# An RWKV scan in chunks of 64 tokens: both directions in one batch, every product 64x64 in two diagonal tiles of the matrix engine

## The chip, the cores and the metric

One core of a Trainium2 chip runs the whole program in one launch. The metric is the device time of that launch in microseconds, the median of three runs.

## The reference

Two transformer-like blocks, one behind the other, over 512 tokens of width 1024, all in float32. The first has an RWKV-7 mixer and a gated linear attention, then a mixture of 32 experts; the second has a gated recurrence, a Hyena convolution, a conformer part and two mixtures of 16 experts. The change touches the RWKV mixer alone:

```python
def rwkv7_bidir_scan(r, w, k, v, kk, b):    # 8 heads of 64; k, w, b per direction
    ...
    def step(s, inp):
        r_t, w_t, k_t, v_t, kk_t, b_t = inp
        sa = jnp.einsum('dbhvk,dbhk->dbhv', s, -kk_t)
        s = s * w_t[..., None, :] + sa[..., None] * b_t[..., None, :] + v_t[..., None] * k_t[..., None, :]
        return s, jnp.einsum('dbhvk,dbhk->dbhv', s, r_t)
    _, ys = lax.scan(step, s0, xs)
    return ys[0] + jnp.flip(ys[1], axis=1)
```

Here w is `exp(-exp(-0.5) * sigmoid(...))`, k_dir is `k * (1 + (a - 1) * k_a)`, b is `kk * a`; the result is normalised per head, gets a bonus from `r * (k_dir[0] + k_dir[1]) * r_k`, and is gated.

## The kernel before, in words

Features lie on the partitions, tokens on the free axis: a tile [128, 4, 512] holds four pairs of heads (partitions 0 to 63 the one head, 64 to 127 the other, called `par` 0 and 1). The stages run one behind the other in blocks, each with a barrier at its end; the order within a block is that of each engine's own instructions, and semaphores join them.

`rwkv_keys` makes kk; `to_tokens` transposes v. Then, for each direction:

- `rwkv_direction` (L636): eight matmuls (L656) with 64 rows make the logits of decay and rate, ACT takes their sigmoid (L663), DVE scales them (L681), sums the decay over each chunk of 128 tokens by sixteen scans (L685), centres the sums on half a chunk (L691), and ACT takes three exponentials (L665 to L676). DVE forms kd and a·kk (L696 to L699) and the products q, b, k (L703 to L706); GpSimd keeps kd_sum (L712, L714) and makes r (L717).
- `to_tokens` transposes b and k (L736, evacuated by L744 and L751).
- `rwkv_scan` (L753) goes over four chunks of 128 tokens. In a chunk the inverse of a triangular 128x128 matrix per head is built up in seven levels of doubling. Jobs, each one PSUM bank, are put into one list. A, N, RB, BT and RK (L835) are products of two of q, r, k, b over 64 rows, four heads each, masked by DVE. At each level l: U = N·X (L839), then X (L843) and Z (L847), which add to one half of X and Z in place. rhs (L854, L855), sa (L861), y (L867 to L869) and S (L875, L876) carry the state; those of the chunk before are put between the levels of the next. PE waits until the job eight places before has left its bank and until the inputs' jobs are evacuated. DVE does all evacuations in list order and waits for its own last one each time (L893 to L925).

`rwkv_output` (L927) then normalises y; DVE multiplies kd_sum by r and r_k there (L978), while GpSimd splits the next projection's weights (L273). ACT takes a square root (L967), DVE the reciprocal (L980).

Float32 products appear in the trace as two MATMUL records each, every one with its own LDWEIGHTS record.

## Time and profile before

| | us |
|---|---|
| median of 3 runs | 3662.59 |
| lowest, highest | 3660.34, 3702.36 |
| profiled execution, its own time | 3687.77 |
| its span, first to last instruction | 3686.0 |
| PE busy (14568 matmul records) | 2898.9 |
| DVE busy | 1643.6 |
| ACT busy | 541.7 |
| GpSimd busy | 369.0 |
| mean granted clock of PE | 0.851 |

Times inside the program are read from the profiled execution, in us from its first instruction. Busy shares are means over very different stages, so a stage is read by its own window. PE is the matmul queue, PEld its weight loads; the clock 1.00 is 2.4 GHz and 0.50 is 1.2 GHz.

### The profile page before, as it was taken

To read this page: it belongs to the slowest core of one execution; us is meant where nothing else is said; L and a number is where in the kernel's file an instruction comes from. 1 tells how busy PE (TensorE), PEld (TensorE's weight loads), DVE (VectorE), ACT (ScalarE), POOL (GpSimd) and SP (SyncE) were. 2 spreads that over 40 slices of the span, in tenths; PEclk is the share of its full clock that TensorE was granted. 3 is DMA by queue.
4 is the path that set the end of the run, shared out by engine and by line. 5 is a ranking of instruction groups with operands and counts; after the bars stand their busy time and mean duration, and the time that the engine had idled before them with its cause. 6 is when DMAs were issued, how large, how long until landed. Compare 5 with 4: busy or idle time off the path is not lost. (4 is left out here: it accounts for less than half of the span.)

```text
span 3686.0 us, 35596 instructions
## 1 busy us (share of the span) xinstructions
PE 2898.9 (79%) x14568; PEld 1854.9 (50%) x14568; DVE 1643.6 (45%) x2393; ACT 541.7 (15%) x742; POOL 369.0 (10%) x143
## 2 busy tenths in 40 slices
PE   5873679969967899996378365689898676798997
PEld 4663378859846545453266134534343454443343
DVE  6967465465553323234577555422121584312123
ACT  2121100010011111111422201200000213100001
POOL 3312010010010000000322223000000230000000
PEclk8986579868977899998689577789999887799998
DMA  5650000000012699993164101279999310699995
GB/s 169 215 181 0 9 1 1 1 1 1 1 46 117 288 411 415 415 410 155 46 217 149 41 0 46 120 316 427 428 428 427 104 54 23 263 427 428 428 427 238
DMA packets 136674, 725.36 MB, mean 197 GB/s; under 512 B 11878, under 2 KB 67174, under 8 KB 99367
## 3 DMA queue, kind: packets, MB, share of 16 engines
q1 hardware_dynamic: 112632, 700.98, 47.0%
q10 hardware_dynamic: 23920, 22.68, 1.9%
q8 instruction: 85, 1.39, 0.2%
q14 instruction: 37, 0.30, 0.0%
HBM read 721.53 MB, written 2.10 MB: 196 GB/s over the span
## 5 line engine op out<-in xcount | busy, mean ns | idle before, releaser
L1631 PE MATMUL ps<-s_c_ring,s_c_XG 128*64 128x512 f32 x2048 | 475.0, 620 | 80.2 <-DMA s_c_ring<-in_exp_w 62.6
L289 PE MATMUL ps<-s_h_part,s_w_hi 128*128 128x512 f32 x944 | 310.5, 412 | 63.9 <-PEq L413 63.0
L1631 PEld LDWEIGHTS ps<-s_c_ring,s_c_XG 128*64 128x64 f32 x2048 | 164.5, 142 | 384.8 <-issue 383.7
L273 POOL TENSOR_TENSOR s_w_lo<-s_w_raw,s_w_hi 128x2048 fp32r<-128x2048 f32 (+1 forms) x46 | 213.1, 4638 | 1279.6 <-ACT s_w_hi L266 1250.3
L1744 DVE TENSOR_TENSOR s_c_hid<-ps,s_c_sil 128x512 f32<-128x512 f32 x32 | 34.3, 1072 | 515.7 <-PE ps L1631 515.7
L289 PEld LDWEIGHTS ps<-s_h_part,s_w_hi 128*128 128x128 f32 x944 | 186.7, 200 | 105.8 <-issue 65.6
L1672 PE MATMUL ps<-s_c_ring,s_c_hidT 128*64 128x512 f32 x1024 | 223.3, 594 | 0.0
L1631 PE MATMUL ps<-s_m_ring,s_m_XG 128*64 128x512 f32 x1024 | 222.9, 593 | 0.0
L345 DVE SCALAR_TENSOR_TENSOR s_mod_acc<-s_mod_w,s_mod_silu,s_mod_acc 128x512 f32<-128x512 f32 x196 | 189.2, 965 | 47.4 <-DMA s_mod_w<-in_w_mod 38.5
L289 PE MATMUL ps<-s_h_part,s_w_lo 128*128 128x512 f32 x472 | 191.8, 406 | 0.0
L289 PE MATMUL ps<-s_src_part,s_w_hi 128*128 128x512 f32 x384 | 123.0, 402 | 42.7 <-DVE s_src_part L1262 29.2
L1631 PEld LDWEIGHTS ps<-s_m_ring,s_m_XG 128*64 128x64 f32 x1024 | 72.9, 137 | 142.7 <-issue 141.6
L266 ACT ACTIVATE s_w_hi<-s_w_raw 128x2048 fp32r<-128x2048 f32 (+1 forms) x46 | 87.1, 1893 | 386.4 <-DMA s_w_raw<-in_w_out 270.3
L1672 PEld LDWEIGHTS ps<-s_c_ring,s_c_hidT 128*64 128x64 f32 x1024 | 72.1, 137 | 137.3 <-issue 136.0
L1756 DVE SCALAR_TENSOR_TENSOR s_c_Y_lo<-ps,s_c_w_slot,s_c_Y_hi 128x512 fp32r<-128x512 f32 x32 | 22.5, 746 | 211.6 <-ACT s_c_Y_hi L1713 211.6
L1672 PE MATMUL ps<-s_m_ring,s_m_hidT 128*64 128x512 f32 x512 | 113.4, 595 | 0.0
L839 PE MATMUL ps<-s_rw_X,s_rw_N 128*128 128x128 f32 x768 | 107.2, 298 | 5.6 <-DVE s_rw_Z L899 5.6
L1744 DVE TENSOR_TENSOR s_m_hid<-ps,s_m_sil 128x512 f32<-128x512 f32 x16 | 17.4, 1088 | 199.2 <-PE ps L1631 199.2
L289 PEld LDWEIGHTS ps<-s_src_part,s_w_hi 128*128 128x128 f32 x384 | 74.6, 195 | 60.6 <-DVE s_src_part L1262 30.8
L839 PEld LDWEIGHTS ps<-s_rw_X,s_rw_N 128*128 128x128 f32 x768 | 101.1, 212 | 7.7 <-DVE s_rw_Z L899 6.3
L289 PEld LDWEIGHTS ps<-s_h_part,s_w_lo 128*128 128x128 f32 x472 | 94.0, 199 | 20.9
L1563 DVE SCALAR_TENSOR_TENSOR s_xT<-ps,s_mod_l,s_xT 128x512 f32<-128x512 f32 x144 | 96.3, 740 | 2.0 <-PE ps L1555 1.8
(584 smaller groups left out, 4716.6 us busy)
## 6 DMA issues: line engine op xcount, KB each, us to landing
s_c_ring<-in_exp_w SPq DMA_DIRECT2D x192, 2048.0 KB, 17.3
s_m_ring<-in_moe_w_gate SPq DMA_DIRECT2D x32, 2048.0 KB, 12.0
s_m_ring<-in_moe_w_up SPq DMA_DIRECT2D x32, 2048.0 KB, 15.3
s_m_ring<-in_moe_w_down SPq DMA_DIRECT2D x32, 2048.0 KB, 12.4
s_mod_w<-in_w_mod SPq DMA_DIRECT2D x112, 512.0 KB, 5.0
s_w_raw<-in_w_in ACTq DMA_DIRECT2D x21, 1024.0 KB, 9.2
s_w_raw<-in_w_out SPq DMA_DIRECT2D x8, 1024.0 KB, 5.5
s_w_raw<-in_cf_w SPq DMA_DIRECT2D x16, 512.0 KB, 5.5
```

The lines of the kernel that those rows point to most:

```text
L266: nc.scalar.activation(self.hi[:, i % 2, :, at], self.raw[:, i % 2, :, at], ACT.Copy).then_inc(hi_done.sem, 1)
L273: nc.gpsimd.tensor_tensor(self.lo[:, i % 2, :, at], self.raw[:, i % 2, :, at], self.hi[:, i % 2, :, at].bitcast(F32), ALU.subtract).then_i ...
L289: last = nc.tensor.matmul(bank, w[a][:, i % 2, k, c0:c0 + P], x[b][:, k, at], start=start, stop=stop)
L345: ins = nc.vector.scalar_tensor_tensor(acc, w, c, acc, ALU.mult, ALU.add)
L839: last = mm(bank[:, h * P:(h + 1) * P], N[:, par, h, :], X[:, par, h, :], start=True, stop=True)
L1563: ins = nc.vector.scalar_tensor_tensor(xT[:, d, :], ps[:, bank, :], out_gate(d), xT[:, d, :], ALU.mult, ALU.add)
L1631: last = nc.tensor.matmul(ps[x * SLOTS:(x + 1) * SLOTS, bank + fh, :], XG[:, k, c0:c0 + SLOTS], w[x][:, at:at + 512], start=(k == 0), stop ...
L1672: last = nc.tensor.matmul(ps[rows, DOWN + half, :], hidT[:, f, rows], w[x][:, at:at + 512], start=(f == 0), stop=(f == nj - 1))
L1744: nc.vector.tensor_tensor(hid_out[:, fh * per:(fh + 1) * per, :], ps[:, UP + fh, :].rearrange("s (p j) -> s p j", j=nj), sil[:, fh * 512:( ...
L1756: nc.vector.scalar_tensor_tensor(Y_lo[:, at], ps[:, DOWN + half, :], w_slot[:], Y_hi[:, at].bitcast(F32), ALU.mult, ALU.subtract).then_inc ...
```

## The change

A chunk has 64 tokens and there are eight steps; the inverse has six levels, the first of them from masks. The backward direction is stored reversed, so both directions are the same program, and a job's eight blocks of 64 columns are (direction, pair of heads). Each block has two products, head 0 from partitions 0 to 63 into PSUM partitions 0 to 63, head 1 from 64 to 127 into 64 to 127. U, X and Z only compute the half that is used, 32 columns, one job per direction. b and k come to token order by products with a diagonal that holds the chunk's total decay; v by products with the identity. ACT evacuates b_tok, k_tok, v_tok, rhs, sa and y of the first four steps; DVE the rest, without waiting for itself; GpSimd makes the diagonals and the decayed state. A semaphore per engine takes the place of the shared ones. `rwkv_prepare` takes the place of both `rwkv_direction`s, `to_tokens` of v, b and k are gone from this part (the function stays for other stages), the multiplication of kd_sum by r and r_k goes from `rwkv_output` to the preparation's end, and X, Z, N, RB, RK and v_tok lie where r, k and kk were.

`rwkv_prepare`, ACT and DVE, for each direction d:

```diff
+                for j in range(2 * CT):
+                    c, name, dst = j % CT, (w0, ka0)[j // CT], (sg, a_)[j // CT]
+                    act.wait_ge(mm_done.sem, m0 + d * 2 * CT + j + 1)
+                    nc.scalar.activation(dst[:, c, :], ps[:, j, :], ACT.Sigmoid, bias=vcol(name, c)).then_inc(*act_out.up())
+                act.wait_ge(act_out.sem, a0 + d * PER_ACT + 2 * CT)
+                act.wait_ge(dve_out.sem, v0 + d * PER_DVE + 1)
+                for c in range(CT):
+                    ins = nc.scalar.activation(kd[:, c, :], a_[:, c, :], ACT.Identity, bias=keep[:, c:c + 1], scale=vcol("rw_k_a", c))
+                ins.then_inc(*act_out.up())
+                act.wait_ge(dve_out.sem, v0 + d * PER_DVE + 2)
+                nc.scalar.activation(flat(ex), flat(cc), ACT.Exp, scale=decay).then_inc(*act_out.up())
+                act.wait_ge(dve_out.sem, v0 + d * PER_DVE + 3)
+                nc.scalar.activation(flat(sg), flat(sg), ACT.Exp, scale=-decay).then_inc(*act_out.up())
+                act.wait_ge(act_out.sem, act_out.n)
+                nc.scalar.activation(flat(cc), flat(cc), ACT.Exp, scale=-decay).then_inc(*act_out.up())
+                act.wait_ge(act_out.sem, act_out.n)
+                ends = cc[:, :, 0:T:RW_CHUNK] if d else cc[:, :, RW_CHUNK - 1:T:RW_CHUNK]
+                to = tot[:, :, d * CT:(d + 1) * CT].rearrange("p n c -> p c n")
+                nc.scalar.activation(to[:, :, ::-1] if d else to, ends, ACT.Copy).then_inc(*act_out.up())
+                if d == 0:
+                    nc.scalar.activation(v_back[:, :, ::-1], v_[:, :, :], ACT.Copy).then_inc(*act_out.up())
...
+                for c in range(CT):
+                    dve.wait_ge(act_out.sem, ad + c + 1)
+                    x, s = (cc[:, c, ::-1], sg[:, c, ::-1]) if d else (cc[:, c, :], sg[:, c, :])
+                    ins = V.tensor_tensor_scan(x, reset, s, 0.0, ALU.mult, ALU.add)
+                ins.then_inc(*dve_out.up())
+                dve.wait_ge(dve_out.sem, vd + 2)
+                V.tensor_tensor(flat(sg), flat(cc), flat(sg), ALU.subtract).then_inc(*dve_out.up())
+                dve.wait_ge(act_out.sem, ad + 2 * CT + 1)
+                vlink(V.tensor_tensor(flat(kd), flat(kd), flat(k_), ALU.mult))
+                V.tensor_tensor(flat(a_), flat(a_), flat(kk), ALU.mult)
+                dve.wait_ge(act_out.sem, ad + 2 * CT + 2)
+                vlink(V.tensor_tensor(k, kd[:, :, :], ex[:, :, :], ALU.mult))
+                V.scalar_tensor_tensor(b, a_[:, :, :], -1.0, ex[:, :, :], ALU.mult, ALU.mult)
+                dve.wait_ge(act_out.sem, ad + 2 * CT + 3)
+                V.tensor_tensor(q, kk[:, :, :], sg[:, :, :], ALU.mult)
+                dve.wait_ge(act_out.sem, ad + 2 * CT + 4)
+                ins = V.tensor_tensor(r, r_[:, :, :], cc[:, :, :], ALU.mult)
+                if d == 1:
+                    vlink(ins)
+                    ins = V.tensor_tensor(flat(kd_sum), flat(kd_sum), flat(kd2), ALU.add)
+                ins.then_inc(*dve_out.up())
+            dve.wait_ge(dve_out.sem, v0 + 2 * PER_DVE)
+            for c in range(CT):
+                V.scalar_tensor_tensor(kd_sum[:, c, :], r_[:, c, :], vcol("rw_r_k", c), kd_sum[:, c, :], ALU.mult, ALU.mult)
```

`rwkv_scan`, the order of the jobs, and the matmuls of the wide and the small ones:

```diff
+jobs = [("A", 0, 0, 0), ("N", 0, 0, 0)]
+for j in range(N_STEP):
+    last = j > 0
+    for l in range(1, TOP + 1):
+        one, two = [], []
+        if l == 1:
+            one, two = [("rhs", j - 1, 0, 0)] if last else [], [("RB", j, 0, 0)]
+        elif l == 2:
+            one, two = [("sa", j - 1, 0, 0)] if last else [], [("BT", j, 0, 0)]
+        elif l == 3:
+            one, two = [("S", j - 1, 0, 0)] if last else [], [("b_tok", j, 0, 0)]
+        elif l == 4:
+            one, two = [("RK", j, 0, 0)], [("A", j + 1, 0, 0), ("N", j + 1, 0, 0)] if j + 1 < N_STEP else []
+        else:
+            one, two = [("k_tok", j, 0, 0), ("v_tok", j, 0, 0)], [("y", j - 1, 0, 0)] if last else []
+        jobs += [("U", j, 0, l), ("U", j, 1, l)] + one
+        for d in range(2):
+            jobs += [("X", j, d, l)] if l < TOP else []
+            jobs += [("Z", j, d, l)]
+        jobs += two
+jobs += [(name, N_STEP - 1, 0, 0) for name in ("rhs", "sa", "y")]
...
+def by_act(job):
+    return job[0] in ("b_tok", "k_tok", "v_tok", "rhs", "sa") or job[0] == "y" and job[1] < N_STEP // 2
...
+                if name in ("A", "N", "RB", "BT", "RK"):
+                    lhs, rhs_ = {"A": (qt, bt), "N": (bt, qt), "RB": (bt, rt), "BT": (kt, qt), "RK": (kt, rt)}[name]
+                    for h, (w, c) in enumerate(blocks):
+                        for r in rows:
+                            last = mm(bank[r, h * C:(h + 1) * C], lhs[r, w, c, at], rhs_[r, w, c, at], start=True, stop=True)
+                elif name in ("b_tok", "k_tok"):
+                    pe.wait_ge(pool_did.sem, 2 + 2 * j + 1)
+                    src = bt if name == "b_tok" else kt
+                    for h, (w, c) in enumerate(blocks):
+                        for r in rows:
+                            last = mm(bank[r, h * C:(h + 1) * C], src[r, w, c, at], diag2[j % 2][r, h, :], start=True, stop=True)
...
+                elif name == "U":
+                    after(*(("N", j, 0, 0) if l == 1 else ("X", j, d, l - 1)))
+                    for c in range(CT):
+                        h = d * CT + c
+                        for r in rows:
+                            last = mm(bank[r, c * (C // 2):(c + 1) * (C // 2)], N[r, h, :], part(X[r, h:h + 1, :], l, 0)[:, 0], start=True, stop=True)
+                elif name == "X":
+                    after("U", j, d, l)
+                    for c in range(CT):
+                        h = d * CT + c
+                        for r in rows:
+                            last = mm(bank[r, c * (C // 2):(c + 1) * (C // 2)], Z[r, h, :], part(U[l][r, h:h + 1, :], l, 0)[:, 0], start=True, stop=True)
+                elif name == "Z":
+                    after("U", j, d, l)
+                    for c in range(CT):
+                        h = d * CT + c
+                        for r in rows:
+                            last = mm(bank[r, c * (C // 2):(c + 1) * (C // 2)], U[l][r, h, :], part(Z[r, h:h + 1, :], l, 1)[:, 0], start=True, stop=True)
...
+                elif name == "y":
+                    after("RB", j, 0, 0)
+                    after("RK", j, 0, 0)
+                    after("sa", j, 0, 0)
+                    for h, (w, c) in enumerate(blocks):
+                        for r in rows:
+                            o = bank[r, h * C:(h + 1) * C]
+                            mm(o, S[r, h, :], rt[r, w, c, at], start=True, stop=False)
+                            mm(o, vt[r, h, :], RK[r, h, :], start=False, stop=False)
+                            last = mm(o, sa[r, h, :], RB[r, h, :], start=False, stop=True)
+                else:
+                    after("b_tok", j, 0, 0)
+                    after("k_tok", j, 0, 0)
+                    after("sa", j, 0, 0)
+                    for h in range(BLK):
+                        for r in rows:
+                            o = bank[r, h * C:(h + 1) * C]
+                            mm(o, k_tok[r, h, :], vt[r, h, :], start=True, stop=False)
+                            last = mm(o, b_tok[r, h, :], sa[r, h, :], start=False, stop=True)
+                last.then_inc(pe_did.sem, 1)
```

GpSimd's and DVE's part of it:

```diff
+        @block.gpsimd
+        def _(pool):
+            for l in range(1, TOP + 1):
+                ins = nc.gpsimd.memset(U[l][:], 0.0)
+            ins.then_inc(pool_did.sem, 1)
+            nc.gpsimd.memset(S2[0][:], 0.0).then_inc(pool_did.sem, 1)
+            pool.wait_ge(pool_did.sem, 2)
+            for j in range(N_STEP):
+                if j >= 2:
+                    pool.wait_ge(pe_did.sem, pe_at[("k_tok", j - 2, 0, 0)])
+                t = tot[:, j, :].unsqueeze(2).to_broadcast([P, BLK, C])
+                nc.gpsimd.tensor_tensor(diag2[j % 2][:], bcast(same, BLK), t, ALU.mult).then_inc(pool_did.sem, 1)
+                if j + 1 < N_STEP:
+                    if j > 0:
+                        pool.wait_ge(dve_did.sem, done_at[("S", j - 1, 0, 0)][1])
+                        pool.wait_ge(pe_did.sem, pe_at[("y", j - 1, 0, 0)])
+                    nc.gpsimd.tensor_tensor(S2[(j + 1) % 2][:], S2[j % 2][:], t, ALU.mult).then_inc(pool_did.sem, 1)
...
+                if name == "A":
+                    vlink(tt(X[:], banked(i), bcast(first, BLK), ALU.mult))
+                    ins = tt(X[:], X[:], bcast(same, BLK), ALU.add)
+                elif name == "N":
+                    tt(N[:], banked(i), bcast(strict, BLK), ALU.mult)
+                    vlink(tt(Z[:], banked(i), bcast(first_t, BLK), ALU.mult))
+                    ins = tt(Z[:], Z[:], bcast(same, BLK), ALU.add)
+                elif name in ("RB", "RK", "BT"):
+                    to, mask = {"RB": (RB, incl), "RK": (RK, incl), "BT": (BT, strict)}[name]
+                    ins = tt(to[:], banked(i), bcast(mask, BLK), ALU.mult)
+                elif name == "U":
+                    mask = level(l).rearrange("p (m b) -> p m b", b=2 ** l).unsqueeze(1).to_broadcast([P, CT, C // 2 ** (l + 1), 2 ** l])
+                    ins = tt(part(U[l][:, mine, :], l, 0), halves(i, l), mask, ALU.mult)
+                elif name in ("X", "Z"):
+                    M = part(X[:, mine, :], l, 0) if name == "X" else part(Z[:, mine, :], l, 1)
+                    ins = tt(M, M, halves(i, l), ALU.add)
+                elif name == "y":
+                    dve.wait_ge(act_did.sem, done_at[("y", N_STEP // 2 - 1, 0, 0)][1])
+                    for w in range(2):
+                        o = y_at(j, w)
+                        ins = tt(o, banked(i)[:, w * CT:(w + 1) * CT, :], o, ALU.add)
...
+                    dve.wait_ge(pool_did.sem, 2 + 2 * (j + 1))
+                    S = S2[(j + 1) % 2]
+                    ins = tt(S[:], banked(i), S[:], ALU.add)
+                ins.then_inc(dve_did.sem, 1)
```

`rwkv_output` loses its four passes:

```diff
-            for c in range(CT):
-                nc.vector.scalar_tensor_tensor(kd_sum[:, c, :], r_[:, c, :], vcol("rw_r_k", c), kd_sum[:, c, :], ALU.mult, ALU.mult).then_inc(*dve_out.up())
```

## Rows read from the trace of the kernel before

**Rows 1.** Windows by stage: us, busy (x records) by engine, PEclk, DMA share.

```profile
436.98:1053.46 616.48, 551.53 (x3952) 483.75 (x3952) 328.45 (x530) 32.49 (x37) 23.36 (x4) 0.83 0.00 1
441.90:477.65 35.75, 11.54 (x16) 4.19 (x16) 29.78 (x29) 12.62 (x13) 10.38 (x2) 0.54 0.00 0
484.36:746.21 261.85, 256.47 (x1920) 230.52 (x1921) 129.70 (x231) 0.01 (x1) 0.00 (x0) 0.88 0.00 1
...
791.68:1053.46 261.78, 256.41 (x1920) 230.41 (x1920) 129.67 (x231) 0.00 (x0) 0.00 (x0) 0.88 0.00 1
```

**Rows 2.** Timeline of the forward scan: start, us, engine, line, [idle <-releaser].

```profile
584.79 1.95 PE L839 MATMUL ps<-s_rw_X,s_rw_N 128*128 128x128 f32 x16
585.06 0.42 DVE L906 TENSOR_TENSOR s_rw_ex<-s_rw_ex,ps 128x256 f32<-128x256 f32 x1 [0.47 <-PE ps L847]
585.96 0.69 DVE L903 TENSOR_TENSOR s_rw_U<-ps,s_masks 128x512 f32<-128x512 f32 x1 [0.47 <-PE ps L839]
...
586.70 0.38 PE L843 MATMUL ps<-s_rw_U,s_rw_ex 128*128 128x128 f32 x1
```

**Rows 3.** PE's timeline, an S job (L875, L876) at full clock.

```profile
572.54 0.34 PE L875 MATMUL ps<-s_rw_sa,s_rw_lw 128*64 128x64 f32 x4
...
573.01 0.33 PE L875 MATMUL ps<-s_rw_sa,s_rw_lw 128*64 128x64 f32 x4
```

**Rows 4.** PE's timeline, an S job at half clock.

```profile
1050.78 0.48 PE L875 MATMUL ps<-s_rw_sa,s_rw_lw 128*64 128x64 f32 x4
...
1051.63 0.48 PE L875 MATMUL ps<-s_rw_sa,s_rw_lw 128*64 128x64 f32 x4
```

**Rows 5.** PE's timeline where A's and N's jobs meet.

```profile
486.02 0.27 PE L835 MATMUL ps<-s_rw_a,s_rw_q 64*128 64x128 f32 x1
486.02 0.27 PE L835 MATMUL ps<-s_rw_q,s_rw_a 64*128 64x128 f32 x1
```

**Rows 6.** PE's timeline, products with 32 moving columns at half clock.

```profile
1195.29 4.48 PE L1362 MATMUL ps<-s_Mboth,s_base 128*128 128x32 f32 x20 [5.99 <-DVE s_Mboth L1403]
```

**Rows 7.** Timeline of the first rwkv_direction.

```profile
441.93 4.71 PE L656 MATMUL ps<-s_proj,s_w2s 64*128 64x512 f32 x8 [1.28 <-PEq L725]
...
448.66 5.16 DVE L685 TENSOR_TENSOR_SCAN s_rw_cc<-s_base,s_rw_lw 128x128 f32<-128x128 f32 x16
...
453.50 0.69 ACT L663 ACTIVATE s_rw_a<-ps,s_vec 128x512 f32<-128x512 f32 x1 [1.02 <-PE ps L656]
...
454.21 1.28 ACT L665 ACT_TABLE_LOAD   x1
...
462.50 2.28 DVE L699 TENSOR_TENSOR s_rw_a<-s_rw_a,s_rw_kk 128x2048 f32<-128x2048 f32 x1
...
468.60 6.58 DVE L704 TENSOR_TENSOR s_rw_a<-s_rw_a,s_rw_ex 128x2048 f32<-128x2048 f32 x1
```

**Rows 8.** Timeline of rwkv_output.

```profile
1060.90 9.41 POOL L273 TENSOR_TENSOR s_w_lo<-s_w_raw,s_w_hi 128x2048 fp32r<-128x2048 f32 x2 [280.42 <-ACT s_w_hi L266]
1061.69 0.69 DVE L976 TENSOR_SCALAR s_gn_sq<-ps 128x512 f32<-128x512 f32 x1 [1.67 <-PE ps L952]
...
1062.30 9.88 DVE L978 SCALAR_TENSOR_TENSOR s_rw_kd_sum<-s_proj,s_vec,s_rw_kd_sum 128x512 f32<-128x512 f32 x4
...
1065.09 0.63 ACT L967 ACTIVATE s_gn_sq<-s_gn_sq 128x512 f32<-128x512 f32 x1
```

**Rows 9.** Groups of GpSimd: busy us, mean ns of one.

```profile
L2253 POOL TENSOR_TENSOR s_hY<-s_hU,s_Ks 128x512 f32<-128x512 f32 x4 | 6.8, 1706 | 0.0
...
L1586 POOL MEMSET s_c_GT<- 128x512 f32 x2 | 1.1, 526 | 0.0
```

**Rows 10.** Windows of PE alone: us, busy (x records), PEclk.

```profile
441.00:444.40 3.40, 2.47 (x6) 1.00 0.01 2
444.40:454.60 10.20, 9.07 (x11) 0.50 0.00 0
...
540.00:550.20 10.20, 10.20 (x47) 0.50 0.00 0
```

More of the change, by code:

```diff
@@ L30 @@
 GLA_CLAMP = 80.0
-LEVELS = 7
+RW_CHUNK, RW_LEVELS = 64, 6
 N_GROUPS, PER_GROUP = 4, 8
@@ L122, in shape_constants @@
     cols.add("base_end", np.zeros((P, 1)))
-    cols.add("strict", np.concatenate([row < col, row > col], axis=1))
     cols.add("incl", np.concatenate([row <= col, row >= col], axis=1))
+    tok, to = row % RW_CHUNK, np.arange(RW_CHUNK)[None, :]
+    cols.add("same64", tok == to)
+    cols.add("strict64", tok < to)
+    cols.add("incl64", tok <= to)
+    cols.add("level0", (tok // 2 == to // 2) & (tok > to))
+    cols.add("level0_t", (tok // 2 == to // 2) & (tok < to))
     levels = []
-    for back in (False, True):
-        for s in (2 ** l for l in range(LEVELS)):
-            lower = (row // (2 * s) == col // (2 * s)) & (row // s > col // s)
-            levels.append(lower.T if back else lower)
+    for s in (2 ** l for l in range(1, RW_LEVELS)):
+        lower = (tok // (2 * s) == to // (2 * s)) & (tok // s > to // s)
+        levels.append(lower[:, (to[0] // s) % 2 == 0])
     cols.add("levels", np.concatenate(levels, axis=1))
+    cols.add("reset", np.tile(np.arange(T) % RW_CHUNK != 0, (P, 1)))
     return cols
@@ L976, in _ @@
                         nc.vector.tensor_scalar(sq[:, 0, :], ps[:, 0, :], 1.0 / RW_HD, RW_GN_EPS, ALU.mult, ALU.add).then_inc(*dve_out.up())
-                        for c in range(CT):
-                            nc.vector.scalar_tensor_tensor(kd_sum[:, c, :], r_[:, c, :], vcol("rw_r_k", c), kd_sum[:, c, :], ALU.mult, ALU.mult).then_inc(*dve_out.up())
                         dve.wait_ge(act_out.sem, a0 + 1)
@@ new lines, in build, with again @@
+                        bufs = {n: sbuf(scan, "rw_" + n, [P, 2, CT, T]) for n in ("q", "r", "k", "b")}
+                        bufs["v_back"] = sbuf(scan, "rw_v_back", [P, CT, T])
+                        bufs["tot"] = sbuf(scan, "rw_tot", [P, T // RW_CHUNK, 2 * CT])
+                        rwkv_prepare(proj, kk, w2, a2, kd_sum, bufs, masks["reset"])
+                        def again(t, n):
+                            return [t.rearrange("p c n -> p (c n)")[:, m * T:(m + 1) * T].rearrange("p (h i) -> p h i", i=RW_CHUNK) for m in range(n)]
@@ new lines, in build @@
+                        old = again(proj[:, 0:8, :], 8) + again(kk[:, :, :], 4)
+                        for n in ("X", "Z", "N", "RB", "RK", "v_tok"):
+                            bufs[n] = [old.pop(), old.pop()]
+                        for n in ("S", "diag"):
+                            bufs[n] = [sbuf(scan, "rw_" + n, [P, 2 * CT, RW_CHUNK]) for _ in range(2)]
+                        bufs["U"] = {l: sbuf(scan, "rw_U", [P, 2 * CT, RW_CHUNK]) for l in range(1, RW_LEVELS)}
+                        for n in ("BT", "rhs", "sa", "b_tok", "k_tok"):
+                            bufs[n] = sbuf(scan, "rw_" + n, [P, 2 * CT, RW_CHUNK])
```

396 lines of the change are left out of this document (141 added, 255 removed).

## The prediction

> **What bounds the kernel now.** I read the core's span first, then the windows by stage, then the timeline of one stretch of the scan, and last the granted clock of single windows. The part that the diff replaces runs from 436.98 to 1053.46 us, 616.5 us in 530 DVE and 3952 matmul records [rows 1]. Of that the two scans are 261.9 and 261.8 us, with PE busy 256 us of each; the first preparation is 35.8 us with DVE busy 30 of it; the second, v's transposes and the two `to_tokens` fill the remaining 57 us. So the scans are PE-bound and the preparations DVE-bound. Each scan is 1920 matmul records, and one 128x128 float32 product is two records: 16 records take 1.95 us, one starts every 0.11 us, and DVE answers 0.47 us after its last evacuation, then PE goes on 0.05 us after DVE [rows 2]. The reader is to see there that evacuations (0.69 us for 512 columns, 0.42 for 256) hide behind the other half of the heads. Nothing else runs: DMA share 0.00 [rows 1]. What a shorter scan saves, the span saves.
>
> **The preparation.** Counted along its longest chain. Forward: eight 64-row matmuls and sigmoids paced by them, 12.3 us (441.9 to 454.2, the same records as now [rows 1, 7]); four ACT Identity passes, 2.5 us (ACT's 0.69 us a pass, a little overlapped; estimate); then six DVE passes over 128x2048 (kd, a·kk, k, b, q, r) at 2.29 us, 13.7 us [rows 7]. The scans and one subtraction lie beside PE, the three exponentials and their table load (1.28 us) beside the DVE passes. Sum 28.6. Backward: PE has finished long before; table and first sigmoid 2.0, four 512-column scans 5.2 (the same 5.16 us as sixteen of 128 [rows 7]), subtraction 2.3, six passes 13.7, the kd_sum addition 2.3, four r·r_k·kd_sum passes over 512 columns, a little over DVE's 0.69 each, 3.0: 28.5. With the block's entry and exit 1.5: 59 us. Ends: 55 if every pass overlaps its neighbour a little, 72 if each direction takes what the first preparation takes now [rows 1]. Two things in my favour are already in the sum: GpSimd leaves this stage, and next to its passes (10.4 us in this stage [rows 1]) DVE's two-SBUF products took up to 6.58 instead of 2.28 us [rows 7]; both `to_tokens` and v's transposes go (into the scan, as products).
>
> **The scan, PE.** One step (64 tokens, both directions) has: wide jobs of 16 products 64x64x64 for A, N, RB, RK, BT, b_tok, k_tok, v_tok, sa, twice that for rhs and S, three times for y: 16 x 16 = 256 products; and 28 small jobs (10 U, 8 X, 10 Z) of 8 products with 32 moving columns: 224. That is 480 products, 960 records; eight steps less the last S: 7616 records, against 3840 now. What does a record cost? Before has no pair of diagonal tiles, but has its two halves. Two column tiles in one bank: the S products (64 output columns, 64 moving) start 16 records in 0.47 us (572.54 to 573.01, as many on the lines left out as on those shown), 0.029 us each, at the full clock [rows 3], and 16 in 0.85, 0.053 each, at the half clock [rows 4]. Two row tiles in different banks: A's and N's records start in the same instant, 486.02 and 486.02, where they meet [rows 5]. So I take 0.029 for a diagonal pair's wide records. A small record streams half as much, but its weights are still 64 columns: the 20 records with 32 moving columns and 128 of weights took 4.48 us at the half clock, 0.22 us each, as long as 128 moving columns need there [rows 6]; weights bound it, and I take 0.029 again. 7616 x 0.029 = 222 us (28 us a step). Ends: 15 us a step (119 us) if a small record cost nothing; 0.11 us per record, the longest stretch that the trace shows at a steady pace [rows 2], would be 838 us.
>
> **The scan, the others.** DVE per step: A's two and N's three passes, RB, RK, BT, S, at 0.69 [rows 2], y half the time, and 28 evacuations of 128 columns, 0.29 us by the line through 0.69 and 0.42: 6.2 + 0.4 + 8.1 = 14.7 us, half of PE's 28. ACT takes five copies, no slower than DVE's: 3.5 us. GpSimd: two 128x512 products at 1.7 us [rows 9]. Only the two additions whose operands are both in SBUF share its port; a DVE pass with a PSUM source was 0.69 us beside GpSimd [rows 8]. Waits: U to X has 0.47 + 0.29 + 0.05 us to cover and U of the other direction (0.46) plus a wide job do so; only the first step lacks the wide jobs; after A and N DVE owes 3.5 us, which is k_tok's and v_tok's time and a little more. I put 1 us a step: 8. Start: the six memsets of 0.53 [rows 9] keep DVE's first evacuation 1.5 us. End: the last rhs, sa and y are bare, 4 us; exit 1.5.
>
> **The clock.** The scan begins after some 30 us in which PE stood. The trace has PE at half clock where its records are sparse: 540.0 to 550.2 holds 47 records in 10.2 us at 0.50, behind rhs, whose products change between 64 and 128 rows; the scan's mean is 0.88 [rows 1, 10]. I let four levels of the first step run at half clock, +13 us, and the rest at full. Scan: 222 + 8 + 1.5 + 5.5 + 13 = 250.
>
> **Elsewhere.** `rwkv_output` loses the four passes of 9.88 us (2.5 each, beside GpSimd's splitting); the reciprocal then waits for ACT's root at 1065.7 instead of starting at 1072.1, when the four are through: 6.3 us less [rows 8]. They cost 3 us in the preparation, counted. The smaller mask load is counted at nothing: it can only save a little at the head.
>
> **Sum.** 616.5 - 59 - 250 = 307.5, with 6.3: 313.8 us. The profiled execution took 3687.8 us (span 3686.0); it becomes 3374. It stands 25 us above the median of 3662.6, so for the median I forecast 3349, say 3350 us.
>
> **A rule against it.** Rows 5 show row tiles together in two banks, and rows 3 column tiles together in one; no row shows two row tiles in one bank, which is what every job does now. The Trainium skill, TensorEngine Tiling (Array Packing), section Gotcha 1: PSUM Pressure, says that different row tiles cannot access the same PSUM bank at once. By that rule the sum would be the serial rival's. Here the two tiles write different partitions, so I hold the rule to be about shared ones.
>
> **Rivals.** (1) The pairs run one after the other. Then a record of 64 columns takes 0.107 us at half clock (twice rows 4), a small one half: 256 x 0.213 + 224 x 0.107 = 78.5 us a step, 621 for all, 641 with waits and ends, and the sum is 616.5 + 6.3 - 59 - 641 = -77: 3740 us, slower. It decides from a mean of 0.143 us a product on ((616.5 + 6.3 - 59 - 20) / 3808), where I have 0.058. For it: the missing row; against: rows 3 and 5. At full clock it would be near 3440. Chance 0.05 slow clock, 0.04 full.
> (2) The clock stays at half: 7616 x 0.053 = 400 instead of 222 + 13: +165, 3515 us. For it: small tiles, half the array, and 441.0 to 444.4 at 1.00 with 64-row products followed by ten us at 0.50 though PE went on [rows 7, 10]; against: two of them together cover all rows, and the scan's column pairs kept the full clock [rows 3]. Chance 0.17.
> (3) PE cannot be fed so fast for long. The trace has 32 records in a row at 0.029 us [rows 3] and then slower ones; at twice that, 0.06, the scan is +235, 3585 us, just beyond 2%. Chance 0.08. The Trainium skill, TensorE: Matmul & The Clock Gate, section "Wait — 56ns, not 53.3ns?", gives about 62 ns per matmul where firmware decodes, by which the sum would be near 3600. The Trainium skill, PSUM — Partial Sum Buffer, section Specifications (TRN2), says that by default TensorE decodes in hardware; no row here shows which holds.
> (4) DVE becomes the bound, if small evacuations cost 0.5 us: 20 us a step still lies below 28; it only adds late waits, 3380, inside my range.
>
> **Chances.** Forecast 0.62, (1) 0.09, (2) 0.17, (3) 0.08, faster than 3310 0.04. The range 3310 to 3560 leaves out (3), the slow (1) and the 0.04. A measurement of this kernel tells about 2%, 73 us. Faster by over 2% (below 3589): all but the slow (1) and half of (3): 0.91; same 0.04, slower 0.05.
>
> **What would show it.** PE with x18264 matmul records. Preparation 59 us without GpSimd; GpSimd in the scan, two passes a step. A wide job of 32 records in 0.93 us, its records in pairs with the same start; a small job of 16 in 0.46. Scan steps of 29 to 30 us with PE busy throughout, granted clock near 1 after the first. Wrong would be: records at 0.05 and more at full clock (1, 3), PEclk 0.5 through the scan (2), DVE as what PE waits for (4), or a preparation over 70 us.

## The result, and the profile after

The kernel after takes 3349.5 us (median of 4 runs, 3341.3 to 3377.6), the one before 3667.4 beside it; the ratio is 0.912, with a 95% interval of 0.906 to 0.917. The forecast was 3350 us. The profiled execution of after took 3377.62 us (span 3375.5), where the prediction had 3374 for the profiled one. Behind that near hit stand an error of 8 us in the sum and 15 us from a stage that the change doesn't touch, and they go opposite ways; the stages show them.

Windows by stage of the kernel after: everything ahead of `rwkv_keys`; `rwkv_keys`; the preparation; the scan; `rwkv_output`; the rest [rows 1]. A window counts each record that lies partly in it.

```profile
0.00:435.90 435.90, 295.05 (x1288) 231.97 (x1288) 284.79 (x331) 85.30 (x99) 101.03 (x33) 0.74 0.36 118
435.90:451.30 15.40, 6.84 (x16) 1.31 (x16) 10.71 (x14) 3.03 (x4) 0.00 (x0) 0.61 0.17 51
451.30:509.60 58.30, 19.18 (x32) 8.07 (x33) 46.30 (x29) 33.50 (x36) 0.01 (x1) 0.56 0.00 0
509.60:752.80 243.20, 237.18 (x7616) 236.40 (x7617) 112.43 (x303) 26.52 (x48) 18.59 (x21) 0.94 0.02 4
752.80:783.30 30.50, 16.23 (x40) 6.03 (x40) 21.88 (x30) 5.74 (x4) 8.97 (x2) 0.76 0.21 69
783.30:3375.50 2592.20, 2038.82 (x9272) 1140.41 (x9272) 993.40 (x1486) 414.59 (x598) 236.22 (x104) 0.88 0.63 258
```

616.5 us have become 58.3 + 243.2 = 301.5. The scan has its 7616 records, PE is busy for 237 of 243 us, DVE for less than half.

DVE's timeline of the scan after. First its evacuations of small jobs at the half clock (519.44, 520.29) and, last, at the full one (737.06, 737.53): PE is what they wait for, one job of 16 records every 0.853 and every 0.466 us, so 0.0533 and 0.0291 us a record. Between them stands A's evacuation in two following steps.

```profile
519.44 0.29 DVE L983 TENSOR_TENSOR s_rw_kk<-s_rw_kk,ps 128x128 f32<-128x128 f32 x1 [0.56 <-PE ps L868]
520.29 0.29 DVE L983 TENSOR_TENSOR s_rw_kk<-s_rw_kk,ps 128x128 f32<-128x128 f32 x1 [0.56 <-PE ps L874]
...
568.79 0.69 DVE L969 TENSOR_TENSOR s_rw_kk<-ps,s_masks 128x512 f32<-128x512 f32 x1 [0.67 <-PE ps L846]
...
597.07 0.69 DVE L969 TENSOR_TENSOR s_rw_kk<-ps,s_masks 128x512 f32<-128x512 f32 x1 [0.67 <-PE ps L846]
...
737.06 0.29 DVE L983 TENSOR_TENSOR s_rw_kk<-s_rw_kk,ps 128x128 f32<-128x128 f32 x1 [0.18 <-PE ps L868]
737.53 0.29 DVE L983 TENSOR_TENSOR s_rw_kk<-s_rw_kk,ps 128x128 f32<-128x128 f32 x1 [0.18 <-PE ps L874]
```

A step takes 28.28 us for 960 records: 0.02946 each, forecast 0.029. The whole list of what PE waited for, from the first small jobs (517 us) to the first product behind the scan, is this (the view of waits, engine PE):

```profile
PE ps L1015 <- PEq L822: 1.1, 1, 1.1
PE ps L892 <- ACT s_rw_rhs L954: 0.8, 1, 0.8
PE ps L900 <- ACT s_rw_sa L954: 0.7, 1, 0.7
```

All three belong to the bare end. Within the steps PE waits for nobody. Ahead of this window it stands once, 3.4 us between N's products and the first U, while DVE works on A and N. PE's timeline of a y job shows the pairs, two records that start at most 0.01 us apart, the next two 0.06 us later (L901 and L902 are the second and third product of a block of y):

```profile
630.22 0.22 PE L901 MATMUL ps<-s_proj 64*64 64x64 f32 x1
...
630.23 0.22 PE L902 MATMUL ps<-s_proj,s_rw_sa 64*64 64x64 f32 x1
```

The scan's windows show the granted clock and the start: A and N and what DVE does with them, then 24 us at the half clock, then full. A and N themselves ran at half; the clock was full from 512.8 to 516.3, nearly all of it time in which PE stood, and fell just as the first U came.

```profile
509.60:516.30 6.70, 3.56 (x64) 3.44 (x64) 4.22 (x5) 0.00 (x0) 6.33 (x9) 0.75 0.01 4
516.30:540.10 23.80, 23.48 (x440) 23.48 (x442) 7.44 (x23) 0.60 (x1) 0.00 (x0) 0.50 0.01 2
540.10:568.80 28.70, 28.70 (x983) 28.65 (x981) 15.34 (x43) 2.99 (x5) 0.00 (x0) 1.00 0.02 5
```

The groups of the scan by form (busy us, mean ns | idle before, releaser) answer to the durations that the prediction took from [rows 2, 9]: 0.29 us for a small evacuation as estimated; the additions with both operands in SBUF 0.78, a little over 0.69; GpSimd's passes 1.04 and 1.11 us instead of 1.7.

```profile
L983 DVE TENSOR_TENSOR s_rw_kk<-s_rw_kk,ps 128x128 f32<-128x128 f32 x144 | 41.4, 287 | 49.4 <-PE ps L868 30.6 <-PE ps L874 18.4
...
L935 POOL TENSOR_TENSOR s_rw_diag<-s_masks,s_rw_tot 128x512 f32<-128x512 f32 x8 | 8.3, 1041 | 0.1
L940 POOL TENSOR_TENSOR s_rw_S<-s_rw_S,s_rw_tot 128x512 f32<-128x512 f32 x7 | 7.7, 1106 | 191.8 <-PE ps L902 191.8
```

The preparation after [rows 7]: ACT's timeline has the forward direction's Identity passes (from 466.05, when its last sigmoid is done), DVE's the first and the last long pass on that direction's chain and the r_k passes.

```profile
466.05 2.93 ACT L714 ACTIVATE s_rw_kd_sum<-s_rw_a,s_rw_keep,s_vec 128x512 f32<-128x512 f32 x4
```

DVE's:

```profile
469.01 2.29 DVE L752 TENSOR_TENSOR s_rw_kd_sum<-s_rw_kd_sum,s_proj 128x2048 f32<-128x2048 f32 x1 [6.19 <-ACT s_rw_kd_sum L714]
...
480.28 2.29 DVE L760 TENSOR_TENSOR s_rw_r<-s_proj,s_rw_cc 128x2048 f32<-128x2048 f32 x1
...
506.24 2.74 DVE L767 SCALAR_TENSOR_TENSOR s_rw_kd_sum<-s_proj,s_vec,s_rw_kd_sum 128x512 f32<-128x512 f32 x4
```

The forward direction takes 31.2 us (451.3 to 482.5), the backward one 26.5. In `rwkv_output` the reciprocal starts 0.03 us after ACT's root (timeline, against [rows 8]):

```profile
764.13 0.63 ACT L1035 ACTIVATE s_gn_sq<-s_gn_sq 128x512 f32<-128x512 f32 x1
764.79 3.35 DVE L1046 RECIPROCAL s_gn_sq<-s_gn_sq 128x512 f32<-128x512 f32 x1 [3.08 <-ACT s_gn_sq L1035]
```

### The profile page after: what moved, and what is told of

It reads as the page before. It is cut to its first block and busy times, and to the rows that moved or that the text cites. A ratio compares the mean times of both kernels' runs of the same rounds, so it can differ in the third digit from the quotient of the medians.

```text
span 3375.5 us, 42404 instructions
## 1 busy us (share of the span) xinstructions
PE 2613.3 (77%) x18264; PEld 1624.2 (48%) x18264; DVE 1469.5 (44%) x2191; ACT 568.7 (17%) x789; POOL 364.8 (11%) x160
## 5 line engine op out<-in xcount | busy, mean ns | idle before, releaser
L1697 PEld LDWEIGHTS ps<-s_m_ring,s_m_XG 128*64 128x64 f32 x1024 | 72.8, 137 | 142.7 <-issue 141.6
L1810 DVE TENSOR_TENSOR s_m_hid<-ps,s_m_sil 128x512 f32<-128x512 f32 x16 | 17.4, 1088 | 199.2 <-PE ps L1697 199.2
L1627 DVE TENSOR_TENSOR s_xT<-ps,s_xT 128x512 f32<-128x512 f32 x136 | 82.9, 678 | 1.6 <-PE ps L1621 1.6
L294 PE MATMUL ps<-s_src_part,s_w_lo 128*128 128x512 f32 x192 | 76.5, 398 | 0.0
```

What stands on the lines that cost most here:

```text
L294: last = nc.tensor.matmul(bank, w[a][:, i % 2, k, c0:c0 + P], x[b][:, k, at], start=start, stop=stop)
L1627: ins = nc.vector.tensor_tensor(xT[:, d, :], ps[:, bank, :], xT[:, d, :], ALU.add)
L1697: last = nc.tensor.matmul(ps[x * SLOTS:(x + 1) * SLOTS, bank + fh, :], XG[:, k, c0:c0 + SLOTS], w[x][:, at:at + 512], start=(k == 0), stop ...
L1810: nc.vector.tensor_tensor(hid_out[:, fh * per:(fh + 1) * per, :], ps[:, UP + fh, :].rearrange("s (p j) -> s p j", j=nj), sil[:, fh * 512:( ...
```

## What the runs scatter by

Ahead of the changed part nothing differs, yet `rwkv_keys` starts at 435.9 us in this profile and at 421.1 in the one of before. Between the experiments below it starts anywhere from 397.8 to 440.4. One stage makes most of the difference, the GLA products just ahead of it. The window over it in before:

```profile
335.30:382.00 46.70, 46.59 (x249) 38.14 (x250) 14.46 (x37) 0.00 (x0) 0.00 (x0) 0.72 0.00 1
```

The same in after:

```profile
336.10:397.00 60.90, 60.81 (x250) 49.43 (x250) 14.71 (x38) 0.00 (x0) 0.00 (x0) 0.52 0.00 1
```

And in the version called full clock from the start below, the second of the two:

```profile
336.40:372.00 35.60, 35.50 (x252) 29.25 (x252) 14.90 (x38) 0.00 (x0) 0.00 (x0) 1.00 0.00 1
```

Some 250 records take 35.6, 46.7 or 60.9 us, at a granted clock of 1.00, 0.72 or 0.52. That is 25 us of scatter, 0.7% of the whole, from one stage that runs now at one clock and now at the other; what decides it there is open. Gains of 10 us are therefore read from the stage in the profile; the medians only bound them.

## Experiments

**One tile at a time.** Every job of the scan first does all products of partitions 0 to 63, then all of 64 to 127:

```
-for h, (w, c) in enumerate(blocks):
-    for r in rows:
+for r in rows:
+    for h, (w, c) in enumerate(blocks):
```

> The kernel after, with the same 7616 products' records in the scan, but in every job first all products of partitions 0 to 63 and then all of 64 to 127, so that neighbours are no longer on different tiles. Theory A (one record of 64 rows keeps its own quarter of the array for about 0.058 us at the full clock, and 0.029 comes only from two neighbours on different tiles running together): a step grows from 28.3 to about 56 us, the scan from 243 to about 460, the whole to about 3570 to 3600 us; somewhat less if PE looks a few records ahead where a job changes tiles. Rival B (0.029 us is what PE needs to issue or load any record of 64 columns, whatever tile it is on): step and time unchanged, 3350 to 3380 us.

Measured: 3718.7 us in a single run, where before took 3667.6 beside it: 1.4% more, less than the 2% that the prediction asks of a difference. The scan itself is beyond doubt. Its second window:

```profile
590.00:1084.60 494.60, 492.10 (x6558) 491.56 (x6556) 94.92 (x252) 23.53 (x43) 12.26 (x12) 0.50 0.01 2
```

A step is 71.2 us and the scan 570.8. Rival B falls. The step is above Theory A's 56 us by a second effect: the clock is at half to the scan's end. So this order loses twice, by tile and by clock; the two are separated below.

**The price of a record.** A block of products ahead of the scan, whose results nobody reads, one pattern behind the other; the first in short:

```
+for i, h, w, c, at in ops(64):
+    for r in rows:
+        mm(ps[r, i // BLK % 8, h * C:(h + 1) * C], bt[r, w, c, at], qt[r, w, c, at], start=True, stop=True)
```

> The kernel after, with a block of products put between the preparation and the scan whose results nobody reads (the scan overwrites them). Each pattern is 128 products of 64 rows (256 records): 64 moving columns in diagonal pairs in one bank; the same with the two tiles in two banks; 32 moving columns; 16; 128; 64 moving with only 32 columns of weights; 64 products on the upper tile and then 64 on the lower; two products on one tile, then two on the other; last 64 products over all 128 rows and columns; before and behind them 320 pairs as the first pattern. Theory A (pairs overlap in one bank; the weights' 64 columns set the pace): one bank and two banks equal at 0.029 us a record, 32 and 16 moving columns also 0.029, 128 moving 0.058, one tile at a time 0.058, full-array products 0.11 a product of two records or more; 32 columns of weights 0.029 if 64 moving set it. Rival B (two row tiles cannot use one bank at once, and the pairs only overlap elsewhere): two banks clearly faster than one. Rival C (a record costs 0.029 to issue, whatever it holds): all of 64 columns or fewer at 0.029, one tile at a time too. The granted clock should be at half at the start, rise within some 25 us of dense pairs, and, if a half-used array lowers it, fall in the stretch on one tile. The whole: 3350 plus the block, 90 to 120 us.

The views of the single lines (record durations, first and last start): 64 moving columns in one bank (L837), in two banks (L840), 32 moving (L843), 32 columns of weights (L852), one tile at a time (L855), two and two (L863), all rows and columns (L865).

```profile
L837 PE MATMUL ps<-s_rw_q,s_rw_b x256: 217/218/219, 510.2 to 517.7; 64*64 64x64 f32 x128
...
L840 PE MATMUL ps<-s_rw_q,s_rw_b x256: 217/218/219, 517.7 to 525.1; 64*64 64x64 f32 x128
...
L843 PE MATMUL ps<-s_rw_q,s_rw_b x256: 192/219/220, 525.2 to 532.6; 64*64 64x32 f32 x128
...
L852 PE MATMUL ps<-s_rw_q,s_rw_b x256: 215/216/240, 558.9 to 566.1; 64*32 64x64 f32 x128
...
L855 PE MATMUL ps<-s_rw_q,s_rw_b x256: 218/218/267, 566.2 to 580.9; 64*64 64x64 f32 x128
...
L863 PE MATMUL ps<-s_rw_q,s_rw_b x256: 217/218/267, 580.8 to 588.4; 64*64 64x64 f32 x128
...
L865 PE MATMUL ps<-s_rw_q,s_rw_b x128: 275/275/323, 588.6 to 602.8; 128*128 128x64 f32 x128
```

By first and last start over 255 gaps: 0.029 in one bank and 0.029 in two, so sharing the bank costs nothing, and rival B falls. 32 moving columns 0.029, 16 the same while the clock was full, and 32 weight columns 0.028: fewer columns buy nothing below the 64x64 pair. One tile at a time 0.058, but two products on one tile and then two on the other 0.030: the pairs needn't be direct neighbours. So rival C falls as well for products on one tile, though 0.028 is the least that any pattern here showed; the Trainium skill, TensorE: Matmul & The Clock Gate, section Wait — 56ns, not 53.3ns?, gives about 25 ns as the least from start to start, near what these rows show. A product over all 128 rows and columns with the same 64 moving takes two records of 0.112, 0.224 us, and does the work of two small ones (0.117 together) and of two that nobody wants. That is what the two tiles are worth per product.

The windows of that block show the clock: its first 3.4 us; what follows; the 32 moving columns; then the later part of the 16 moving columns, which begin at 532.6, and the first of the 128, which begin at 543.4. Between the rows shown, up to 536.1, the clock was 1.00.

```profile
471.30:474.70 3.40, 3.28 (x62) 3.31 (x64) 0.00 (x0) 0.00 (x0) 0.00 (x0) 0.51 0.03 7
474.70:490.00 15.30, 15.30 (x530) 15.30 (x528) 0.00 (x0) 0.00 (x0) 0.00 (x0) 1.00 0.02 4
...
525.10:532.60 7.50, 7.50 (x266) 7.50 (x261) 0.00 (x0) 0.00 (x0) 0.00 (x0) 1.00 0.02 4
...
536.10:546.30 10.20, 10.20 (x171) 10.20 (x170) 0.00 (x0) 0.00 (x0) 0.00 (x0) 0.50 0.01 3
```

Pairs with 64 moving columns had the full clock 3.4 us after they began, though PE had stood for tens of us before. Pairs with 32 kept it for their 7.5 us. With 16 it fell though PE never paused, and came back at 546.3, 3 us after the 128 columns began.

The scan behind the block, which is that of the kernel after, is worth a look too: it takes 236.3 us instead of 243.2. PE comes to it with 37 us of pairs at the full clock, and A and N run at full. The clock still falls while PE stands ahead of the first U (4.9 us there), but it is back 7.8 us after that U, where the kernel after needs 23.8. The whole run took 3502.3 us.

**PE kept busy until the scan.** 110 pairs nobody reads, behind the backward sigmoids:

```
+pe.wait_ge(act_out.sem, a0 + PER_ACT + 9)
+for i in range(110):
+    for r in (slice(0, 64), slice(64, 128)):
+        nc.tensor.matmul(ps[r, ...], w2[r, ...], a2[r, ...], start=True, stop=True)
```

> The kernel after, with 110 pairs of products (440 records) whose results nobody reads, issued on PE in the preparation once the backward direction's sigmoids are done, so that PE is busy until the scan begins. Theory A (the first 30 us of the scan run at half clock only because PE stood before): the scan begins at the full clock, its first step takes about 10 us less, all later work is unchanged, about 3340 us where the kernel after has 3350. Rival B (the clock waits for something else, such as the small tiles of the first step without wide jobs): first step unchanged at half clock until about 30 us in. Rival C: the 440 records end too early, PE stands again, and nothing is gained.

Windows over the unread products' second part, A and N, what DVE does with them, and the first step from its first U on:

```profile
494.60:505.50 10.90, 10.02 (x344) 9.88 (x340) 10.79 (x6) 1.70 (x2) 0.00 (x0) 1.00 0.02 5
508.20:511.60 3.40, 3.20 (x60) 3.23 (x62) 0.78 (x2) 0.00 (x0) 3.15 (x7) 0.50 0.01 2
511.60:515.10 3.50, 0.34 (x10) 0.20 (x6) 3.47 (x4) 0.00 (x0) 3.19 (x3) 0.99 0.00 0
515.10:538.90 23.80, 23.51 (x440) 23.51 (x442) 7.41 (x23) 0.60 (x1) 0.00 (x0) 0.50 0.01 3
```

The whole took 3385.8 us, within what after itself scatters by. The clock was full from 494.6 until the scan's start at 508.2; but the unread products ended early, PE stood 3.8 us, and A and N ran at half again. It rose at 511.6, and at 515.1, after PE had stood 3.5 us ahead of the first U, it fell; the first step has the same 23.8 us at half as in after, and the scan is 243.5 us. So the long stand before the scan isn't what the first step's half clock hangs on, and Theory A, which was also the prediction's reason ("some 30 us in which PE stood"), falls in that form. In part this is rival C: the fill left a gap, and the short stand between N and U was never filled. The fall comes in or right behind that stand in after, in this run and behind the measured block. What keeps the clock at half for so long behind it is the next question.

**64 moving columns in the small jobs.** They cost PE nothing by the rows above; DVE takes its half from the wider result:

```
-mm(bank[r, c * (C // 2):(c + 1) * (C // 2)], N[r, h, :], part(X[r, h:h + 1, :], l, 0)[:, 0], ...)
+mm(bank[r, c * C:(c + 1) * C], N[r, h, :], X[r, h, :], ...)
```

> The kernel after itself, unchanged, on the same chip as the three that follow: about 3350 us, scan 243 us with its first 30 us at half clock. It is the measure for them.

> The kernel after, with 64 moving columns instead of 32 in all U, X and Z products; DVE takes the half that it needs, so all results are the same. The measured block showed 32 and 64 moving columns at the same 0.029 us a record, the clock full 3.3 us after dense pairs with 64 moving columns began, and the half clock under pairs with 16. The first step of the kernel after is small products alone, at half clock for 24 us though PE never stood. Theory A (few moving columns keep the clock down there, not the stand before): the clock rises within some 5 us of the first U, the first step loses about 10 us, all other steps stay at 28.3 us, the whole 8 to 12 us less than the kernel after. Rival B (the stand before, or the time since it, sets the clock): the first step as before, the whole unchanged. Rival C (the full clock makes DVE's answers the pace there, 0.17 us behind each small job): the gain is only a few us.

After itself: 3377.9 us (median of 6), ratio to before 0.917 (0.911 to 0.923). With 64 columns: 3351.7, 0.911 (0.906 to 0.917). The intervals overlap; the windows decide:

```profile
516.90:520.30 3.40, 3.03 (x56) 3.04 (x58) 1.05 (x4) 0.00 (x0) 0.00 (x0) 0.50 0.00 0
520.30:535.30 15.00, 14.88 (x501) 14.61 (x500) 7.99 (x25) 0.60 (x1) 0.00 (x0) 1.00 0.02 4
```

The clock rises 3.4 us after the first U instead of 24. From A's first evacuation to the second 22.7 us instead of 31.4, all later steps 28.28, the scan 234.4 instead of 243.3: 8.9 us for nothing but wider reads. Theory A, with two things to add. First, its first step isn't "small products alone": by the list of jobs a wide one (RB, BT, b_tok) ends each of the first three levels, and of the 440 records at half clock 320 are small. Later steps have two wide jobs or more to a level, and their 32 columns keep the full clock. Second, 32 columns don't always need 24 us: behind the measured block it was 7.8. So wide reads bring the clock back soon, in the one profile taken; with 32 columns it took 7.8 or about 24 us, and what decides between these is open.

**One tile at a time, with 64 moving columns.** The first experiment and the last one together:

> All products of a job on the upper tile, then all on the lower, as in the first run, and all small products with 64 moving columns. In the first run the scan was at half clock to its end and a step took 71.2 us; the measured block had 64 moving columns one tile at a time at 0.0575 us a record with the full clock kept for its 15 us. Theory A (one tile at a time costs the factor of nearly two; the half clock came from the small products' 32 columns on half the array): clock full from the second step at the latest, a step of 960 records at 0.05 to 0.0575, 48 to 56 us, scan about 430 us, the whole about 3540 to 3570 us. Rival B (half the array alone keeps the clock down in the long run): a step of 85 to 100 us at half clock, the whole above 3800 us.

```profile
492.00:823.80 331.80, 329.29 (x7459) 328.85 (x7456) 106.68 (x293) 26.51 (x48) 12.25 (x12) 0.98 0.01 3
```

3453.2 us; the clock is full from 492, 14 us into the scan, until its bare end, and a step is 41.67 us. Rival B falls. My 48 to 56 was too dear: where a job ends on one tile and the next begins on the other, PE's timeline has their records alternating, so part of them still run together. So of the first experiment's step, 71.2 us, the order costs 13.4 over after's 28.3, and the half clock the other 29.5.

**Full clock from the start.** Besides the wide small jobs, unread pairs up to the scan's start and between N and U, and DVE waits for GpSimd's zeros only at the first U:

> The run before this one, and besides: 175 pairs of products that nobody reads behind the backward sigmoids in the preparation, until the scan begins; 40 more between the first N and the first U; and DVE waits for GpSimd's zeros only ahead of the first U evacuation, not ahead of A's. Theory A (the clock follows how densely PE streams): full clock from some 6 us after the first dummy products on to the end of the scan; A, N and the first small jobs at full clock too, 11 to 16 us less than the kernel after in all. Rival B: dummy products collide with the preparation's DVE or ACT passes, or delay the scan's start, and eat the gain: the same time as the kernel after.

3366.4 us (0.913, 0.907 to 0.919). The clock was full throughout the scan and the scan 232.9 us. Here the short stand ahead of the first U is filled as well, but together with the 64 columns, so the run doesn't tell the two apart. The preparation took 63.0: rival B in part, since 700 unread records outlast the stage. With fewer:

> As the run with the full clock throughout, with as many unread products as fit: 138 pairs in the preparation instead of 175, and 18 between N and U instead of 40. In that run they outlasted what they were to fill: PE was still at them 5 us after DVE's last pass of the preparation (the stage took 63.0 us instead of 58.2), and some 2 us after DVE had evacuated N. Theory A (nothing else was wrong with it): preparation back at 58.3 us, scan 230 to 231 us, full clock from some 6 us after the first unread product to the scan's end; together 289 us where the kernel after has 301.5. The whole 12 us under the kernel after, which is less than its runs differ among themselves. Rival B: the clock falls where the fill now leaves a gap, and the first step costs some us more.

```profile
459.00:475.30 16.30, 14.69 (x504) 14.55 (x500) 15.61 (x10) 4.23 (x4) 0.00 (x0) 1.00 0.01 4
475.30:707.70 232.40, 229.05 (x7688) 227.08 (x7689) 110.86 (x303) 26.51 (x48) 18.64 (x21) 1.00 0.02 4
```

3344.5 us (0.907, 0.902 to 0.913), the lowest median of all, though the interval overlaps that of after. Preparation and scan take 58.3 + 232.4 = 290.7 us, 10.8 less than after; I had said 289, and two of its steps took 28.8 instead of 28.28, which stays unexplained. Its profiled run also had the GLA stage at full clock, by chance.

**DVE takes ACT's copies.** b_tok, k_tok, v_tok, rhs and sa become DVE copies:

```
-return job[0] in ("b_tok", "k_tok", "v_tok", "rhs", "sa") or job[0] == "y" and job[1] < N_STEP // 2
+return job[0] == "y" and job[1] < N_STEP // 2
```

> The kernel after, with ACT's five copies of a step (b_tok, k_tok, v_tok, rhs, sa) given to DVE; ACT keeps only y's. Theory A (PE is the bound and DVE has half a step free): DVE's busy time in a step grows by about 3.5 us to 18, the step by 0 to 1 us where a copy stands ahead of a small evacuation in DVE's queue, the whole by 0 to 8 us. Rival B (the small evacuations have no slack, so that any further DVE work delays the chain of U, X and Z): the step grows by 3 us or more, the whole by 25 us or more.

Two steps (windows):

```profile
605.60:662.20 56.60, 56.48 (x1902) 56.00 (x1901) 32.76 (x84) 1.26 (x4) 4.08 (x4) 1.00 0.02 4
```

DVE is busy 32.8 of 56.6 us, where after has 27.2 in a window as long; the steps are 28.28, 28.7 and 28.57 and then 28.28 again, the scan 244.4 us, the whole 3384.2. Theory A: DVE's half has room.

**The cover taken away.** Within a level U, X, Z of one direction and then of the other:

```
-jobs += [("U", j, 0, l), ("U", j, 1, l)] + one
 for d in range(2):
+    jobs += [("U", j, d, l)]
     jobs += [("X", j, d, l)] if l < TOP else []
     jobs += [("Z", j, d, l)]
+    jobs += [] if d else one
```

> The kernel after, with the jobs of a level in another order: U, X and Z of the forward direction, then the level's wide job, then U, X and Z of the backward direction. X then stands directly behind the U that it needs. Theory A (the other direction's U is what hides the answer of 0.47 + 0.29 + 0.05 us): PE stands about 0.8 us behind each of the 10 U jobs of a step, the step grows from 28.3 to about 36 us, the scan from 243 to about 300, and the whole to 3405 to 3440 us. Rival B (the products' own queue hides it): no change. If the many stands pull the clock down, it is worse: a step of 45 us and more, the whole above 3500.

The waits of PE over two steps (73.1 us; total, times, longest):

```profile
PE ps L869 <- DVE s_rw_U L981: 7.5, 16, 0.6
PE ps L875 <- DVE s_rw_U L981: 5.3, 4, 2.3
```

3437.1 us, a step mostly 36.6 (two of them 38), the scan 314.0. The waits come to 6.4 us a step; together with smaller gaps the other direction's U is worth 8.3 us a step, and the batch of two directions is what provides it. The mean granted clock from 525.3, 32 us into the scan, was still 0.97.

**GpSimd beside the preparation.** Six of its products over 128x2048, which nobody reads:

```
+for i in range(6):
+    ...
+    nc.gpsimd.tensor_tensor(flat(mix[:, 0:CT, :]), flat(kk), flat(v_), ALU.mult).then_inc(extra.sem, 1)
```

> The kernel after, with six products of GpSimd over 128x2048 (kk by v, into y's place, which nobody reads before the scan overwrites it) beside the preparation. The profile of before had DVE products of two operands in SBUF at up to 6.58 instead of 2.28 us beside GpSimd. Theory A (they share a port, and leaving GpSimd out of the stage is worth its price): the DVE passes under GpSimd's six grow to 3 to 6 us each, and the preparation from 58 to 75 us or more, the whole by as much; the scan is unchanged. Rival B (the long passes of before had another cause): preparation 58 us as before.

```profile
451.01 32.65 POOL L696 TENSOR_TENSOR s_mix<-s_rw_kk,s_proj 128x2048 f32<-128x2048 f32 x6 [123.07 <-SPq L690]
...
479.20 6.62 DVE L760 TENSOR_TENSOR s_rw_kd_sum<-s_rw_kd_sum,s_proj 128x2048 f32<-128x2048 f32 x1
485.85 2.29 DVE L761 TENSOR_TENSOR s_rw_a<-s_rw_a,s_rw_kk 128x2048 f32<-128x2048 f32 x1
```

The preparation takes 72.8 us instead of 58.3, the whole 3393.0. The two long DVE passes that lie beside GpSimd take 6.4 and 6.6 us, the first one behind it 2.29 again: it is the neighbour, not the pass. The four scans, which the expectation left out, take 17.4 us together, where each took 1.23 alone; with them and the first long pass the second one starts 28.2 us into the stage, in after 17.7. Theory A, though the stage stays a little under the 75 us that I gave it.

## Why the prediction was right

- **Records and their price** (7616 x 0.029 = 222): right. 0.02946 x 7616 = 224.4. The step that carried the forecast, that diagonal pairs run together in one bank as rows 3 and 5 show it for other pairs, holds; the rule of the Trainium skill weighed against it (TensorEngine Tiling (Array Packing), Gotcha 1: PSUM Pressure) does not bind here, where the two tiles write different partitions: one bank and two banks cost the same. Tiles that write the same partitions were not tried. Rival 1 is out. So is rival 3: 0.02946 holds for 200 us on end.
- **Small record equals wide record**: right in size. The reason given, weights of 64 columns, isn't the whole of it: with 32 columns of weights a record is no cheaper either.
- **Waits, 8 us**: wrong, within the steps there are none. This is the term that was mis-sized. I charged 1 us a step for A and N and for gaps of the cover, but k_tok, v_tok, y and the other direction's U cover all of it; taken away, it costs 8.3 us a step.
- **Clock, 13 us for four levels of the first step**: right in place and size (440 records in 23.8 us, where 0.02946 each would be 13.0, so 10.8 lost), wrong in cause. It was not the long stand before the scan (39.1 us, not some 30): with that mostly filled nothing changed. The fall follows the 3.4 us in which PE stands ahead of the first U, and with 32 moving columns the clock took 24 us to come back, with 64 it took 3.4. That the block's run needed only 7.8 with 32 is not explained; so the size was right partly by luck. Rival 2, the half clock throughout, did not come; the first experiment shows that another order of the same products brings it.
- **Start and end** (1.5 + 5.5): the stretch from the block's start to the first U is 6.7 us, of which 64 records at full clock would be 1.9, so 4.8; the end has 1.5 us of bare waits and 1.1 of exit. The scan's sum was 250, measured 243.2.
- **Preparation, 59 us**: measured 58.3, from two errors. Forward 31.2 instead of 28.6: the sigmoids are paced by 64-row products, and these had a later clock than in before (14.7 instead of 12.3). Backward 26.5 instead of 28.5: for the most part because ACT's table load is done while DVE still works, and the scans take 4.6 instead of 5.2. The gain from GpSimd's absence is shown by the last experiment.
- **`rwkv_output`, 6.3 us**: 37.2 to 30.5, 6.7.
- **DVE 14.7 us a step and hidden**: 13.6 (27.2 for two steps), hidden but for about 1 us of the scan even at 16.4. Rival 4 is out.
- **The sum**: 616.5 - 301.5 + 6.7 = 321.7 us saved where I had 313.8, 8 us more. The scan gives 7 of them: the waits 8 and the clock 2 less than forecast, the records 2 and the start and end about 1 more. The profiled run lost 14.8 us ahead of `rwkv_keys`, almost all in the GLA stage, which has nothing to do with the change. That the median came out within 1 us of the forecast is luck: the same kernel's six later runs have a median of 3377.9. The stage-by-stage sum is what bears the forecast out, not the total.

## What to carry to other kernels

Where a batch of small independent products keeps only a part of a 128x128 array busy, pack them onto diagonal tiles and order them so that neighbours alternate between tiles; here a record of either half costs 0.029 us, one tile at a time 0.058. Fewer moving or weight columns than 64 gained nothing more per record, so count records, and try the moving columns that small products get for free: here the clock came back sooner with them, and that was worth 9 us. Two independent chains interleaved in one queue hide the answer of the evacuating engine wholly; that cover, not DVE's share of busy time, is what to protect.

## What the runs showed of the hardware that I had not expected

- PE busy without a gap is not enough for the full clock. In pairs it was full with 64 moving columns and fell with 16; with 32 it stayed full for 7.5 us in the block, but in the first step of after, where it had fallen, it stayed at half for 24 us (7.8 behind the block). With one tile at a time it was full with 64 and half with 32 in the small jobs. It rose 3.4 us after pairs with 64 began.
- At the half clock a pair's record takes 0.0533 us, not twice 0.0291: 1.8 times.
- One stage, at full clock in one run and at half in another, makes 25 us of scatter between runs of the same program.
- GpSimd's 128x512 products with a mask or a state take 1.04 and 1.11 us, where the nearest row of before had 1.7.
